# Second attention of a two-layer encoder: score and value rounds, turns and copies put in another order

## What is computed

```python
z = rms_norm(h, mix_norm[1]) @ w_in[1]
z_mix, z_mem = z[..., :768], z[..., 768:]
q = partial_rope(rms_norm(z_mix.reshape(B, S, 12, 64), attn_q_norm), cos, sin)
y_mix = banded_sink_attention(q, k_shared, v_shared, sinks)   # 12 heads, 4 K/V heads, chunks of 64, window 128
y_mem = memory_attention(z_mem.reshape(B, S, 4, 64), mem, ...) # 4 heads over 256 memory rows
h = h + concatenate([y_mix, y_mem]) @ w_out[1]
h = swiglu_half_step(h, ffn2_norm[1], ...)                     # "ffn3" in the kernel
```

## Time and profile before

| | |
|---|---|
| median of three timed launches | 926.96 us (926.58 to 927.1) |
| the profiled launch | 926.93 us |
| its span, first to last instruction | 925.1 us |
| granted TensorE clock, mean | 0.999 of full speed |
| PE busy | 916.2 us (99% of the span) |
| DVE busy | 633.3 us (68%) |
| ACT busy | 500.2 us (54%) |
| POOL busy | 50.6 us (5%) |

### The profile page before, as it was taken

One profiled execution on the slowest core, in us unless ns is written; L12 is line 12 of the kernel. 1 busy time (PEld: TensorE's weight loads), 2 busy tenths in 40 slices (PEclk: granted clock), 3 DMA queues, 4 the chain that ended last, 5 costly groups with the idle time before them and its releaser, 6 DMA issues.

```text
span 925.1 us, 15140 instructions
## 1 busy us (share of the span) xinstructions
PE 916.2 (99%) x5076; PEld 775.4 (84%) x5076; DVE 633.3 (68%) x967; ACT 500.2 (54%) x748; POOL 50.6 (5%) x85
## 2 busy tenths in 40 slices
PE   8999999999999999999999999999999999999998
PEld 5888888888888888888888888888877788888887
DVE  5866566586667856666777856666878777565664
ACT  6744454465646454454465545445676565454542
POOL 2020020003000000000000000000121000000000
PEclk9999999999999999999999999999999999999999
DMA  8877656547146656556465765665444277566551
GB/s 249 299 226 232 193 168 215 183 136 227 48 129 197 221 182 202 188 174 206 137 186 179 230 198 166 217 187 173 149 134 122 62 228 227 181 187 198 169 172 46
DMA packets 136867, 167.03 MB, mean 181 GB/s; under 512 B 10776, under 2 KB 101632, under 8 KB 136832
## 3 DMA queue, kind: packets, MB, share of 16 engines
q1 hardware_dynamic: 135472, 164.67, 56.2%
q0 software_dynamic: 1184, 1.83, 0.8%
q10 hardware_dynamic: 176, 0.07, 0.0%
HBM read 165.48 MB, written 1.05 MB: 180 GB/s over the span
## 4 chain that ended last, share of the span: by engine, by line
PE 94%; DVE 3%; ACT 1%; issue 1%; POOL 0%; ACTq 0%; POOLq 0%
PE ps L1616 29%; PE ps L1617 17%; PE ps L1786 8%; PE ps L1784 8%; PE ps L1782 8%; PE ps L1676 5%; PE ps L1678 5%; PE ps L1677 5%; PE ps L1619 4%; PE ps L1574 1%; DVE w_lo L1058 1%; PE ps L1966 1%; PE ps L1911 0%; PE ps L1880 0%; PE ps L2008 0%
## 5 line engine op out<-in xcount | busy, mean ns | idle before, releaser
L1616 PE MATMUL ps<-mainT,w_hi 128*128 128x512 f32 x1206 | 425.8, 395 | 1.0 <-DVE gate_up_f L1144 1.0
L1058 DVE TENSOR_TENSOR w_lo<-w_raw,w_hi 128x1024 fp32r<-128x1024 f32 x296 | 350.7, 1221 | 42.2 <-ACT w_hi L678 41.8
L1617 PE MATMUL ps<-mainT,w_lo 128*128 128x256 f32 x1378 | 372.0, 280 | 0.0
L678 ACT CAST w_hi<-w_raw 128x1024 fp32r<-128x1024 f32 x296 | 299.5, 1047 | 31.0 <-PE ps L1619 11.3
L1616 PEld LDWEIGHTS ps<-mainT,w_hi 128*128 128x128 f32 x1206 | 226.1, 188 | 51.7 <-DVE gate_up_f L1144 1.2
L1617 PEld LDWEIGHTS ps<-mainT,w_lo 128*128 128x128 f32 x1378 | 260.1, 189 | 7.1
L733 ACT COPY gate_up_f<-ps 128x512 f32<-128x512 f32 x88 | 51.2, 582 | 111.6 <-PE ps L1619 106.2
L1142 DVE TENSOR_TENSOR gate_up_f<-ps,gate_up_f 128x256 f32<-128x256 f32 x88 | 37.2, 423 | 98.3 <-ACT gate_up_f L733 98.2
L1782 PE MATMUL ps<-w_hi,actT_hi 128*128 128x512 f32 x320 | 98.7, 390 | 0.4 <-DVE sideT_lo L1096 0.4
L1786 PE MATMUL ps<-w_hi,actT_lo 128*128 128x512 f32 x320 | 98.9, 390 | 0.0
L1784 PE MATMUL ps<-w_lo,actT_hi 128*128 128x512 f32 x320 | 98.8, 390 | 0.0
(11 more groups left out here) (224 smaller groups left out, 838.4 us busy)
## 6 DMA issues: line engine op xcount, KB each, us to landing
w_raw<-in_ffn_w_gate_up_dram SPq DMA_DIRECT2D x352, 256.0 KB, 4.0
w_raw<-in_ffn_w_down_dram SPq DMA_DIRECT2D x176, 256.0 KB, 3.4
w_raw<-in_w_in_dram SPq DMA_DIRECT2D x32, 256.0 KB, 3.4
w_raw<-in_w_out_dram SPq DMA_DIRECT2D x32, 256.0 KB, 3.3
w_raw<-in_w_mem_kv_dram SPq DMA_DIRECT2D x16, 256.0 KB, 3.2
w_raw<-in_w_kv_dram SPq DMA_DIRECT2D x8, 256.0 KB, 3.4
ycat<-in_mem_dram SPq DMA_DIRECT2D x1, 1024.0 KB, 7.5
out_dram<-h SPq DMA_DIRECT2D x4, 256.0 KB, 2.0
```

What stands on the lines that cost most here:

```text
L678: ins = nc.scalar.copy(half(w_hi[s], b), half(w_raw[s], b))
L1058: ins = nc.vector.tensor_tensor(half(w_lo[s], b), half(w_raw[s], b), half(w_hi[s], b).bitcast(F32), ALU.subtract)
L1616: pe.matmul(dst[:, :, tokens], wh, both[:, k, :, tokens], start=start, stop=False)
L1617: mm = pe.matmul(dst[:, 0, tokens], wl, both[:, k, 0, tokens], start=False, stop=False)
```

## The change

Only the order of instructions changes, in the second attention, on PE, DVE and ACT. No instruction is added or removed.

```diff
@@ ACT: after z_copy(1, 1, 1) and query_squares(1, 1)
             exponentials(4)
+            exponentials(5)
             query_copy(1, 1)
-            exponentials(5)
             high_unit("out1", 2)
             exponentials(6)
             split("Y1", 0, 1)
-            high_unit("out1", 3)
+            high_unit("out1", 3, (0,))
             exponentials(7)
+            high_unit("out1", 3, (1,))
@@ DVE: attention_split_out
-                probs_copy(7)
+                output(7)
                 low_unit(name, 0, (0,))
                 residual(r, None, 0, 0)
-                output(7)
                 low_unit(name, 0, (1,))
@@ DVE
             maxima(2)
             maxima(3)
             low_unit("z1b", 1)
+            probs_copy(2)
             kv_copy(*mkv1, 1)
             dve.wait_ge(mkv_ready, 2 * NT)
             head_sums("mk1")
-            probs_copy(2)
             head_scale("mk1").then_inc(head_ready, 1)
             output(2)
             low_unit("out1", 0)
...
             maxima(4)
+            maxima(5)
             query_turn(1, 1)
-            maxima(5)
             query_sums(1, 1)
             probs_copy(4)
+            probs_copy(5)
             output(4)
             low_unit("out1", 2, (0,))
-            probs_copy(5)
             maxima(6)
+            output(5)
             low_unit("out1", 2, (1,))
-            output(5)
             split("Y1", 0, 1)
             maxima(7)
             probs_copy(6)
-            low_unit("out1", 3, (0,))
+            probs_copy(7)
             output(6)
-            low_unit("out1", 3, (1,))
+            low_unit("out1", 3)
@@ PE: attention_out_ends
-                out_part(1, 1, 1, 1, turning(after, k5=(1, 0)))
+                out_part(1, 1, 1, 1, turning(after, k6=(1, 0)))
@@ PE: second_values, the hook of z1b for t = 1
-                if k == 1:
+                if k == 2:
                     turn_probs(3)
-                elif k == 2:
                     turn_heads(3)
-                elif k == 3:
+                elif k == 4:
                     pe.wait_ge(o_ready, 3)
                     turn_y(1, 0, 0)
-                elif k == 4:
                     values(3)
                 elif k == 5:
                     pe.wait_ge(headT_ready, 4)
                     turn_query(1, 0)
-                elif k == 7:
-                    pe.wait_ge(o_ready, 4)
-                    turn_y(1, 1, 0)
@@ PE: around out1
+            pe.wait_ge(o_ready, 4)
+            turn_y(1, 1, 0)
             pe.wait_ge(qT_ready, 3)
             scores(4)
-            def part_00(k):
-                if k == 1:
-                    scores(5)
-                elif k == 3:
-                    turn_query(1, 1)
+            scores(5)
             def part_01(k):
                 if k == 0:
+                    turn_query(1, 1)
                     turn_probs(4)
                 elif k == 2:
+                    turn_probs(5)
                     values(4)
             def part_10(k):
                 if k == 0:
-                    turn_probs(5)
-                elif k == 1:
                     pe.wait_ge(qT_ready, 4)
                     scores(6)
-                elif k == 2:
                     values(5)
-                elif k == 3:
-                    pe.wait_ge(o_ready, 6)
-                    turn_y(1, 0, 1)
             def part_11(k):
                 if k == 1:
                     turn_probs(6)
                 elif k == 3:
+                    turn_probs(7)
                     values(6)
             def end_00(k):
-                if k == 5:
-                    turn_probs(7)
+                if k == 6:
+                    values(7)
             def end_01(k):
-                if k == 4:
-                    values(7)
-                elif k == 6:
+                if k == 5:
                     pe.wait_ge(o_ready, 8)
                     turn_y(1, 1, 1)
...
             out_part(1, 1, 0, 0, part_10)
+            pe.wait_ge(o_ready, 6)
+            turn_y(1, 0, 1)
             scores(7)
```

More of the change, by code:

```diff
@@ L2156, in part_11, with end_01 @@
                 elif k == 3:
+                    turn_probs(7)
                     values(6)
             def end_00(k):
+                if k == 6:
+                    values(7)
+            def end_01(k):
                 if k == 5:
-                    turn_probs(7)
-            def end_01(k):
-                if k == 4:
-                    values(7)
-                elif k == 6:
                     pe.wait_ge(o_ready, 8)
                     turn_y(1, 1, 1)
-            out_part(1, 0, 0, 0, part_00)
-            pe.wait_ge(qT_ready, 3)
+            out_part(1, 0, 0, 0)
             out_part(1, 0, 1, 0, part_01)
             out_part(1, 1, 0, 0, part_10)
+            pe.wait_ge(o_ready, 6)
+            turn_y(1, 0, 1)
             scores(7)
```

## The result

The changed kernel takes 928.44 us (median, 928.1 to 928.8) against 926.97 (926.4 to 927.1) for the kernel before: a ratio of 1.0017, with a 95% interval of 1.001 to 1.0024. That is 1.5 us slower. The profiled execution took 928.10 us, its span 926.3; the profiled one of before took 926.93, so the two traces differ by 1.17 us and the medians by 1.47.

What follows compares the result with a forecast made beforehand. PE, busy in 99% of the span, was taken as the bound. A delay of 1.6 us, less 0.17, plus 0.2, gave 1.6, taken as 1.5: 926.96 + 1.5 = 928.5 us, range for 8 in 10 926.2 to 929.5.

Steps and rivals of the forecast that it cites:

- rival A: The forecast: DVE's delay reaches PE at values(3), turn_query(1, 1) and turn_probs(7); 928.5 us, range 927.3 to 929.2; chance 0.55.
- Step 2: At values(3): copies of pT start at 695.83, PE waits twice, and its 0.7 us lead becomes a 0.7 us delay.
- rival B: Faster: no loss at values(3), later releases come in time; 925.3 or 924.7 us; chance 0.15 including a milder 926.4 form.
- Step 1: At turn_heads(3): head_scale lands at 693.04, PE goes on at 693.1, its lead shrinking to 0.5 us.
- Step 3: At turn_query(1, 1): DVE late, maxima(5) ahead of the query turn; PE waits 1.0 us, delay 1.3 at out1's second bank.
- the 1.59 us: Delay on DVE behind head_scale because probs_copy(2) no longer fills the time in which POOL works on the roots.
- Steps 4 and 5: turn_y(1, 0, 1)'s split comes late for out11, delay 0.9 us; then turn_probs(7)'s second half waits, delay 1.6 us.
- PE's own order: Second attention on PE: scores and values side by side and grouped turns save 0.5 to 1.3 us, taken as 1.1.
- rival C: Slower: drain stays between unlike tiles, turns beside tiled matmuls save nothing; order gives 0.5 us, not 1.1; 929.1 us; chance 0.2.
- Step 7: turn_h(1, 0) a triple later loses its 0.3 us wait for h; the wait moves to ffn3's start, +0.2 us.
- my own test: Between 690 and 740 us: waits as forecast and time above 929 would mean PE's own order gave under 1 us.
- the 1.3 of old waits: PE's idle time before the change at values(2), turn_y(1, 0, 1), 730.27 and turn_h(1, 0): together 1.3 us to win.

Runs made afterwards that it cites:

- the gap partly filled: Changed kernel with output(2), which reads PSUM, put on DVE between the key sums and head_scale: 927.97 us.
- copies-back experiment: Changed kernel with probs_copy(2) put back on DVE behind kv_copy and the key sums: 927.80 us.
- query-turn experiment: Changed kernel with query_turn(1, 1) ahead of maxima(5) on DVE again: 928.05 us.
- regrouped order: Changed kernel with scores and values regrouped on PE, probs_copy(3) in DVE's gap, out1's low parts and ACT's high parts later: 924.04 us.

## Why the prediction was right, and where only its sum was

The time came as forecast (928.5 against 928.44), and so did rival A's places: no idle time at values(2), DVE idle for 2.04 us (forecast 2.1), waits in values(3), at turn_query(1, 1), in turn_probs(7) and at ffn3. Set against before, with the 0.53 us of the earlier start taken out, PE is 0.74 us late behind values(3) (697.22 + 0.53 - 697.01; forecast 0.7) and 1.39 late at the second bank of out1 (forecast 1.3). Point by point:

- **Step 2 is shown**, by the copies moved alone (+0.75 us) and by the gap partly filled (-0.5 us). That rival B would decide at the second copy of pT for round 3 holds: in the changed kernel it lands at about 696.5, in this trace's earlier time, and PE had been there at 695.0.
- **Step 1** was right: about 0.3 us of waiting at turn_heads(3). It is no loss of its own: without it PE would have stood 0.3 us longer in values(3).
- **Step 3 had the right size and the wrong cause.** I put the 0.6 us that this step adds down to the 1.59 us, by which DVE would be free for maxima(4) only at 703.0. In the copies-back experiment, without that delay, maxima(4) starts at 701.71 instead of 702.54, and scores(4) at 700.25 instead of 701.07: both 0.8 earlier, and the wait stays at 0.8. In the changed kernel the split ahead of maxima(4) comes 1.28 us behind turn_y(1, 1, 0) (700.54 to 701.82), with the copies back 1.25: the backlog is 0.03 us by then. What PE waits for is maxima(5), now ahead of the query turn, as the query-turn experiment shows: without it the turn is written at 705.51 and PE comes for it at 705.89. That term was in my sum, and so was the start of maxima(4) (703.0, measured 702.54 + 0.53 = 703.07); what was wrong is what holds that start, which is PE, late behind values(3), and not work queued on DVE. So the delay of 1.59 us costs PE time once, in values(3), and not three times as A says. The 0.8 to 0.9 us that the rest of the change costs do not hang on it.
- **Steps 4 and 5** were right in mechanism, and somewhat small in the delay. The wait for the split is 0.34 us. In turn_probs(7) the second half goes at 722.18, 0.66 us behind the end of the first (721.16 + 0.36 = 721.52), of which the view flags 0.42; the forecast was 0.69 (721.76 to 722.45). The delay behind scores(7) is 719.05 - 717.83 = 1.2 instead of 0.9: the wait is as forecast, but PE comes to turn_y(1, 0, 1) at 716.52 + 0.53 = 717.05 and not at 716.8. DVE's row for that split in the changed kernel shows that no backlog is left there either:

```profile
717.77 0.69 DVE L1097 TENSOR_TENSOR yT_lo<-ps,yT_hi 128x512 fp32r<-128x512 f32 x1 [2.23 <-ACT yT_hi L719]
```

- **PE's own order was mis-sized, the way rival C has it.** Like tiles beside each other gave 0.30 and a slow triple, as taken. Unlike tiles, scores(6) beside values(5), run from 711.63 + 0.23 = 711.86 to 713.64, 1.78 us. Apart they took 0.70 + 1.17 = 1.87 (triple's last start + 0.23 to the next triple, in the rows of before below): 0.09 and a slow triple are saved, not 0.43. The regrouped order bears it out: values(6) beside values(7), like tiles, take 1.63 us (720.74 + 0.23 = 720.97 to 722.60) against 0.72 + 1.17 = 1.89 apart, while values(5) ahead of scores(6), unlike tiles, save nothing and scores(6) ahead of scores(7) 0.09. And a group of turns ahead of a tiled group holds the latter until 0.53 us after its start (700.54 to 701.07), where a triple follows after 0.35 and a tiled group starts 0.09 behind a triple: 0.18 is paid, about what a slow triple (0.08) and that entry (0.09) save. Turns in front of turns, at 706.45 and 706.95, are 0.50 apart behind a wait, and 0.43 in the query-turn experiment, where nothing waits (705.89 to 706.32): 0.08 over the 0.35, as much as the slow triple costs. So turns won nothing, and the order gave about 0.41 + 0.20 = 0.6 us instead of 1.1. The Trainium skill, page "TensorEngine Tiling (Array Packing)", section "Key Properties", says that a change of tiling mode drains TensorE; the two pairs agree, 0.30 us for like tiles against 0.09 for unlike. PE's timeline of the kernel before, around scores(6) and values(5):

```profile
711.46 0.40 PE L1678 MATMUL ps<-w_hi,yT_lo 128*128 128x512 f32 x1
...
712.39 0.50 PE L1676 MATMUL ps<-w_hi,yT_hi 128*128 128x512 f32 x1
...
712.97 0.39 PE L1678 MATMUL ps<-w_hi,yT_lo 128*128 128x512 f32 x1
...
714.37 0.50 PE L1676 MATMUL ps<-w_hi,yT_hi 128*128 128x512 f32 x1
```

- **Step 7 is not settled**: the wait at ffn3's tile 1 is there, 0.36 us, but it took the place of 0.3 us, and its net price is below what the times tell.
- **What stays open**: of the 0.85 us that the rest of the change costs, one run shows 0.4 (the query turn). The waits for the split and in turn_probs(7) are read from the trace alone; no run puts turn_y(1, 0, 1) or turn_probs(7) back by itself.

Why then was the sum right? By my own test (waits as forecast and an own order of under 1 us) the time should have passed 929, as in C. The test can be made with numbers: A's delay of 1.6 us, the 1.3 of old waits and 1.1 of order imply 4.0 us of new waits and restarts. The traces give 1.76 + 1.28 + 0.6 = 3.6, of which 2.97 are flagged, 0.3 stand at turn_heads(3), and the rest is in starts that the view does not flag. (By starts throughout, the new waits come to 4.1 us and the old ones to the 1.8 given above; 4.1 - 1.8 - 0.6 = 1.7, which closes the sum.) So both terms were too large by 0.4 to 0.5 us and cancelled. In part that is no accident: a PE that comes later to a release waits less for it. And the 1.76 us of the traces is more than the 1.47 of the medians, so the last 0.3 us of agreement is luck.

## What to carry to other kernels

A wait of the bounding engine is removed only if what is moved to remove it does not itself cover another engine's latency: ask of each moved instruction what idle time it filled where it stood. Before putting a later wait down to an earlier delay, look for an idle moment of the releasing engine in between; at such a moment the delay is gone. In these traces grouping array-tiled matmuls paid where the tiles are alike, and a gap of VectorE behind which GpSimd works was worth filling only with work that reads PSUM.

## What was not expected of the hardware

A small GpSimd instruction can be held for as long as a VectorE instruction runs. The instruction of 0.20 us (L600) occurs eight times; three of them in the changed kernel's trace, POOL's timeline:

```profile
213.19 1.10 POOL L600 TENSOR_SCALAR head_ms<-head_ss 128x8 f32<-128x8 f32 x1 [8.07 <-DVE head_ss L1258]
...
667.60 0.63 POOL L600 TENSOR_SCALAR head_ms<-head_ss 128x8 f32<-128x8 f32 x1 [6.17 <-DVE head_ss L1295]
...
699.12 0.20 POOL L600 TENSOR_SCALAR head_ms<-head_ss 128x8 f32<-128x8 f32 x1 [7.37 <-DVE head_ss L1295]
```

and the instruction that DVE begins behind the sums in each case:

```profile
213.02 2.35 DVE L1059 TENSOR_TENSOR w_lo<-w_raw,w_hi 128x1024 fp32r<-128x1024 f32 x2
...
667.43 2.73 DVE L1064 SCALAR_TENSOR_TENSOR w_lo<-w_raw,gain_col,w_hi 128x512 fp32r<-128x512 f32 x4
...
698.95 0.68 DVE L1379 TENSOR_TENSOR ycat<-ps,den 128x512 f32<-128x512 f32 x1
```

It is 1.10 us behind a low part of 128x1024, whose two inputs lie in SBUF, 0.63 behind one of 128x512, and 0.20 behind an output that reads PSUM. The roots (L601) took 1.64 us at 699.40, although DVE began a pair of low parts at 699.55, but 2.50 at 214.37, where the second low part of the pair at 213.02 was already running, and 2.04 at 668.31, under one of the short low parts. VectorE was not held in turn: its pair at 699.55 took 2.35 us, as the pair at 693.00 did with GpSimd idle. The Trainium skill, page "GPSIMD Engine Reference", section "1. Specifications", says that GpSimd shares its SBUF interfaces with VectorE and contends with VectorE instructions of two SBUF inputs; the rows agree, and add that an instruction of GpSimd is held where it begins under one of VectorE, not where it is under way. The trace of the kernel before has it too (L600 takes 1.10 us at 213.68), and in the earlier trace rows the copies that covered the roots read PSUM.
